# Order of the roundings at the heads of the stages, a shorter choice of expert groups, the first weight chunk in halves, and bias transfers one per chunk

## What is computed

```python
def first_block(x, ...):                       # per layer
    x = x + 0.5 * swiglu(rms_norm(x, ffn1_norm), w_gate, w_up, w_down)        # hidden width 2816
    h = rms_norm(x, mix_norm)
    ... = split(h @ w_in)                      # 5656 columns
    y_nsa = nsa_attention(...)                 # compressed, selected, windowed, with the relative bias
    y_sb  = stick_breaking_attention(...)
    y_swa = swa_sink_attention(...)            # with the relative bias
    x = x + (g0 * (y_nsa @ w_up_nsa) + g1 * (y_sb @ w_up_sb) + g2 * (y_swa @ w_up_swa)) @ w_out
    x = x + 0.5 * swiglu(rms_norm(x, ffn2_norm), ...)

def second_block(x, mem, ...):                 # per layer
    h = concat(gla_group(x @ w_in ...), sgu_group(...)) @ w_out
    x = layer_norm(DN_ALPHA * x + h)
    x = layer_norm(DN_ALPHA * x + mem_xattn(x, mem, wq, wk, wv, wo))
    x = layer_norm(DN_ALPHA * x + grouped_moe(x, ...))

def grouped_moe(x, w_router, b_router, w_gate, w_up, w_down):
    scores = softmax(x @ w_router + b_router)  # 16 experts in 4 groups of 4
    group_score = sum of the two largest scores of each group
    g_sel = argmax(group_score)                # the first of equal ones
    top_w, top_i = top_k(scores of the group g_sel, 2); top_w = top_w / sum(top_w)
    y = sum over the two experts: top_w * (silu(x @ w_gate[e]) * (x @ w_up[e])) @ w_down[e]
```

## Time and profile before

| | us |
|---|---|
| runs | 2324.76, 2325.26, 2319.07 |
| median | 2324.76 |
| the profiled execution | 2323.54 |
| its span in the trace | 2321.7 |
| PE busy | 2270.3 |
| DVE busy | 1598.3 |
| ACT busy | 1245.1 |
| POOL busy | 48.4 |

### The profile page before, as it was taken

The page is one execution under the profiler, slowest core; times in us unless marked ns, Lnnn a source line. Parts: engine busy times, 40 slices in busy tenths (PEclk is TensorE's granted clock), DMA queues, the critical chain, the costliest instruction groups (busy, mean ns, idle before and its releaser), DMA issues.

```text
span 2321.7 us, 31646 instructions
## 1 busy us (share of the span) xinstructions
PE 2270.3 (98%) x13500; PEld 1974.2 (85%) x13500; DVE 1598.3 (69%) x1535; ACT 1245.1 (54%) x1272; POOL 48.4 (2%) x67
## 2 busy tenths in 40 slices
PE   7999999999999999999999999999999999899998
PEld 6888989788888889897888999888888998688886
DVE  5765755777477558556764656688887666688887
ACT  4444634554354446444443545577776545467775
POOL 1000100000000001000000000000000000000000
PEclk9999999999999999999999999999999999899999
DMA  9655443456555554445655554599997554599995
GB/s 236 199 185 178 147 136 130 156 187 194 182 181 182 190 172 129 148 145 170 193 182 189 172 180 165 174 342 348 369 345 278 173 182 147 184 346 344 347 370 184
DMA packets 309793, 490.96 MB, mean 211 GB/s; under 512 B 15472, under 2 KB 205088, under 8 KB 309648
## 3 DMA queue, kind: packets, MB, share of 16 engines
q1 hardware_dynamic: 305696, 475.35, 60.9%
q0 software_dynamic: 3104, 10.38, 1.8%
q10 hardware_dynamic: 848, 3.15, 0.4%
HBM read 487.40 MB, written 1.44 MB: 211 GB/s over the span
## 4 chain that ended last, share of the span: by engine, by line
PE 92%; DVE 4%; ACT 2%; issue 1%; DMA 1%; ACTq 0%; DVEq 0%
PE PS L679 20%; PE PS L680 20%; PE PS L683 19%; PE PS L752 13%; PE PS L755 7%; PE PS L1372 1%; ACT RH L1532 1%; PE PS L975 1%; PE PS L940 1%; DVE RL L2024 1%; DMA RINGS<-ffn_w_up 1%; PE PS L914 1%; PE PS L699 1%; PE PS L925 1%; DVE X L2393 1%
## 5 line engine op out<-in xcount | busy, mean ns | idle before, releaser
L2024 DVE TENSOR_TENSOR RL<-RINGS,RH 128x2048 fp32r<-128x2048 f32 x448 | 1017.3, 2273 | 487.3 <-ACT RH L1532 484.8
L1532 ACT ACTIVATE RH<-RINGS 128x2048 fp32r<-128x2048 f32 x448 | 850.7, 1900 | 474.1 <-PE PS L683 449.6
L679 PE MATMUL PS<-RH,HTS 128*128 128x256 f32 (+1 forms) x1696 | 548.3, 334 | 0.4 <-DVE HTS L2006 0.4
L680 PE MATMUL PS<-RH,HTS 128*128 128x256 f32 (+1 forms) x1696 | 537.8, 328 | 0.0
L752 PE MATMUL PS<-HTS,RH 128*128 128x512 f32 x1384 | 416.7, 397 | 7.4 <-ACT RH L1532 7.4
L683 PE MATMUL PS<-RL,HTS 128*128 128x256 f32 (+1 forms) x1696 | 400.0, 326 | 0.0
L679 PEld LDWEIGHTS PS<-RH,HTS 128*128 128x128 f32 x1696 | 320.4, 189 | 32.6 <-issue 2.5
L680 PEld LDWEIGHTS PS<-RH,HTS 128*128 128x128 f32 x1696 | 321.5, 190 | 28.0
L683 PEld LDWEIGHTS PS<-RL,HTS 128*128 128x128 f32 x1696 | 289.5, 189 | 31.1 <-DVE RL L2024 0.4
L752 PEld LDWEIGHTS PS<-HTS,RH 128*128 128x128 f32 x1384 | 249.0, 189 | 55.6 <-issue 6.2
L755 PE MATMUL PS<-HTS,RL 128*128 128x256 f32 x1408 | 284.3, 281 | 0.4 <-DVE RL L2024 0.4
(11 more groups left out here) (434 smaller groups left out, 2534.7 us busy)
## 6 DMA issues: line engine op xcount, KB each, us to landing
RINGS<-w_in SPq DMA_DIRECT2D x64, 1024.0 KB, 5.3
RINGS<-w_gate SPq DMA_DIRECT2D x64, 1024.0 KB, 5.3
RINGS<-w_up SPq DMA_DIRECT2D x64, 1024.0 KB, 5.3
RINGS<-w_down SPq DMA_DIRECT2D x64, 1024.0 KB, 5.3
RINGS<-ffn_w_gate SPq DMA_DIRECT2D x44, 1024.0 KB, 5.4
RINGS<-ffn_w_up SPq DMA_DIRECT2D x44, 1024.0 KB, 5.3
RINGS<-ffn_w_down SPq DMA_DIRECT2D x44, 1024.0 KB, 4.9
RINGS<-w_out SPq DMA_DIRECT2D x16, 1024.0 KB, 4.9
```

Source lines behind the costliest of these rows:

```text
L679: mm(dst, a_[0], b_[0], start=start, stop=False)
L680: mm(dst, a_[0], b_[1], start=False, stop=False) if left else mm(dst, a_[1], b_[0], start=False, stop=False)
L1532: A(splits.buffer(RH, RH3)[:, 0:width], RINGS[:, slot, 0:width], ACT.Copy).then_inc(wh_ready, 1)
L2024: TTn(RL[:, slot, 0:width], RINGS[:, slot, 0:width], splits.buffer(RH, RH3)[:, 0:width].bitcast(F32), ALU.subtract).then_inc(wl_ready, 1)
```

## The change

1. **Start.** The first chunk is loaded in two transfers: k = 0..3 (`first_loaded`) and k = 4..7 (`ring_full[0]`). DVE rounds the first half itself, ahead of its activation rests, and raises `first_rounded`; ACT rounds only the second half (`split_first`). PE waits for `first_rounded` at k = 0 and for `wh_ready` at k = 4. ACT runs a Silu on one number after issuing x.
2. **Bias.** Each of the eight transfers waits for one more chunk done, from the seventh on. The row of the bias is made ahead of PE's other small products, so that one semaphore serves both.
3. **Rows of X in halves.** Row tile 1 is written as columns 0..511 (`x_left`) and 512..1023 (`x_rows`), at all places; PE's transposes of tile 1 wait for `x_left`, and for `x_rows` ahead of the third bank.
4. **Layer columns.** In block 1 those of layer 1 are copied within the second feed-forward stage of layer 0. In block 2, the copy and two memsets stand behind the activation rests and a weight split.
5. **Roundings.** At the head of the memory attention of layer 1 and of both routings, ACT does its activation copies ahead of one of the roundings that stood before them.
6. **Routing.** The group is chosen by maxima and minima of the exponentials as they are, without the division; the comparisons come behind `oh_ready`, the gates between the seats of groups 1 and 2. The seats of group 0 need one linked step less.
7. **End.** Row tile 1 is stored in two transfers of 256 KB.

```diff
@@ SP, load
+                if ring.n == 1:
+                    dst, half = shape_fn(RINGS[:, slot, :]), K // 2
+                    sp.dma_start(dst[:, 0:half, :], src[:, 0:half, :]).then_inc(first_loaded, 16)
+                    sp.dma_start(dst[:, half:K, :], src[:, half:K, :]).then_inc(ring_full[slot], 16)
+                    return
@@ POOL
                     for q in range(0, P, COPIES):
+
+                        pool.wait_ge(chunks_done, SLOTS + 7 + q // COPIES)
                         nc.gpsimd.dma_start(BIAS[q:q + COPIES, :, :], ...)
@@ PE, to_column_parts
-                pe.wait_ge(wh_ready, splits.v + splits.n)
+                opening = ring.n == 1
+                if opening:
+                    pe.wait_ge(first_rounded, 1)
+                else:
+                    pe.wait_ge(wh_ready, splits.v + splits.n)
...
                     for k in range(K - 1):
+                        if opening and k == K // 2:
+                            pe.wait_ge(wh_ready, splits.v + splits.n)
@@ PE, transpose_halves
-                pe.wait_ge(rows, first + 1)
+                if left is not None:
+                    pe.wait_ge(*left)
+                else:
+                    pe.wait_ge(rows, first + tail)
                 for b in range(4):
-                    if b == 2 and parts:
-                        pe.wait_ge(rows, first + 2)
+                    if b == 2 and left is not None:
+                        pe.wait_ge(rows, first + tail)
@@ ACT
+            def split_first():
...
+                act.wait_ge(ring_full[slot], ahead.full())
+                act.wait_ge(first_rounded, 1)
+                A(splits.buffer(RH, RH3)[:, half:SLOT], RINGS[:, slot, half:SLOT], ACT.Copy).then_inc(wh_ready, 1)
...
+            act.wait_ge(zeroed, 2)
+            A(EPS[:, 1:2], EPS[:, 0:1], ACT.Silu)
...
                     split()
-                    split(back=3)

                 ht_copy(tr2(l, 3), HT)
+                split(back=3)
                 chunk()
...
+            act.wait_ge(x_left, last_rows + 1)
+            act.dma_start(out_view[:, 1, 0:512], X[:, 1, 0:512]).then_inc(out_stored, 16)
+            act.wait_ge(x_rows, 2 * last_rows + 2)
+            act.dma_start(out_view[:, 1, 512:D], X[:, 1, 512:D]).then_inc(out_stored, 16)
@@ DVE
+                if l + f == 0:
+                    dve.wait_ge(first_loaded, 16)
+                    V.tensor_copy(RH[:, 0, 0:SLOT // 2], RINGS[:, 0, 0:SLOT // 2]).then_inc(first_rounded, 1)
                 ht_copy(tr1(l, 4 * f), HT, gains, bank=low)
...
-                V.scalar_tensor_tensor(X[:, 1, :], half_rows(1, low), SMALL[:, 7:8], X[:, 1, :], ALU.mult, ALU.add).then_inc(x_rows, 1)
+                for at, made in ((0, x_left), (512, x_rows)):
+                    part = X[:, 1, at:at + 512]
+                    V.scalar_tensor_tensor(part, half_rows(1, low)[:, at:at + 512], SMALL[:, 7:8], part, ALU.mult, ALU.add).then_inc(made, 1)
```

More of the change, by code:

```diff
@@ L818, in transpose_rows, with transpose_halves @@
                     last.then_inc(tr_ready, 1)
-            def transpose_halves(src, n, rows, first, upper=None, bank=0, parts=False):
+            def transpose_halves(src, n, rows, first, left=None, tail=1, upper=None, bank=0):
                 pe.wait_ge(ht_l, n * 4 + 4)
@@ L871, in swiglu @@
                     pe.wait_ge(consts_loaded, 16 * NLOAD)
+                    mm(PS[0:12, low + 3, :], RB, HOTR, start=True, stop=True)
                 for t in range(T):
@@ L874, in swiglu @@
                 last.then_inc(spread_ready, 1)
-                if l + f == 0:
-                    mm(PS[0:12, low + 3, :], RB, HOTR, start=True, stop=True).then_inc(hot_ready, 1)
                 for j in range(1, FP):
@@ L2594, in _ @@
                 dve.wait_ge(rt_exp, l + 1)
-                link(V.tensor_reduce(SMALL[:, 374:376], r3, AX.X, ALU.add))
-                link(V.reciprocal(SMALL[:, 376:378], SMALL[:, 374:376]))
-                link(TTn(r3, r3, spread(SMALL[:, 376:378], 2, NE), ALU.mult))
+                pairs = R.rearrange("p (g j i) -> p g j i", j=2, i=2)
+                top, low = (RTC[:, 16 * i:16 * i + 16].rearrange("p (g j) -> p g j", j=2) for i in range(2))
+                first, less, rest, second = (RTC[:, 32 + 8 * i:40 + 8 * i] for i in range(4))
+                TTn(top, pairs[:, :, :, 0], pairs[:, :, :, 1], ALU.max)
+                link(TTn(low, pairs[:, :, :, 0], pairs[:, :, :, 1], ALU.min))
+                TTn(first, top[:, :, 0], top[:, :, 1], ALU.max)
+                TTn(less, top[:, :, 0], top[:, :, 1], ALU.min)
+                link(TTn(rest, low[:, :, 0], low[:, :, 1], ALU.max))
+                link(TTn(second, less, rest, ALU.max))
+                link(TTn(SMALL[:, 448:456], first, second, ALU.add))
+                gs = SMALL[:, 448:456].rearrange("p (t g) -> p t g", t=2)
+                link(V.tensor_reduce(SMALL[:, 456:458], gs, AX.X, ALU.max))
+                eq = SMALL[:, 460:468].rearrange("p (t g) -> p t g", t=2)
+                before = RTN.rearrange("p (t g) -> p t g", t=2)
+                TTn(eq, gs, spread(SMALL[:, 456:458], 2, 4), ALU.is_equal)
+                link(TTn(before[:, :, 1], gs[:, :, 0], SMALL[:, 456:458], ALU.is_equal))
+                TTn(before[:, :, 2], eq[:, :, 0], eq[:, :, 1], ALU.max)
+                link(V.tensor_reduce(before[:, :, 3], eq[:, :, 0:3], AX.X, ALU.max))
+                TTn(OH, eq, before, ALU.is_gt).then_inc(oh_ready, 1)
                 r4 = R.rearrange("p (g i) -> p g i", i=4)
@@ L2646, in _ @@
                 for g in range(1, NG_):
-                    seats(g)
+                    if g == 2:
+                        gates()
+                    seat(g, 1)
+                    seat(g, 0).then_inc(seat_ready, 1)
                 wait_apart(dve, crowd_known, l + 1, consts_loaded, 16 * NLOAD)
```

105 lines of the change are left out of this document (56 added, 49 removed).

## The result

| | runs | median us | mean us | lowest to highest us |
|---|---|---|---|---|
| before | 5 | 2323.66 | 2322.7 | 2319.07 to 2325.26 |
| changed | 5 | 2309.93 | 2309.6 | 2308.47 to 2310.14 |

The ratio of changed to before is 0.9947, with a 95% interval of 0.9936 to 0.9958: the changed kernel is 10 to 15 us faster. The forecast was 2314.0, the range 2309.0 to 2320.5. The direction is right, and the time lies in the range, but near its lower end. By the medians the gain is 13.7 us, 3.5 more than the sum of 10.2, and more than the sum of the upper bounds, 12.7.

A forecast was written before the change was run, and what follows sets the result against it. PE, busy 98% of the span, bounds the kernel, so only its 51.4 us idle can shrink. Terms 2.0 + 3.3 + 2.3 + 1.9 + 0.65 = 10.2 us gave 2313.3 to 2314.6, stated 2314.0; range 2309.0 to 2320.5.

The forecast's parts named there:

- sum of 10.2: Whole kernel: gains of 2.0 start, 3.3 bias, 2.3 stage heads, 1.9 layer 1 routing and 0.65 tail, in us.
- Start, 2.0: First chunk: PE starts near 9.75, products with the rest begin at 14.4 instead of 16.88; 2.0 us gained.
- case (a): Rival at the start, chance 0.22: low PE clock takes gain back, start worth 1.0 instead of 2.0; time 2316.
- Bias, 3.3: Bias transfers spread one per load from chunk 7: PE no longer falls dry, 3.3 us gained, bounds 2.3 and 3.3.
- slack of 14.9 us: Weight stream: a load may take about 14.9 us before PE waits.
- price per transfer, 1.5: Bias transfers: eight cost a load 11.9 us, so one costs 1.5 and a load takes 6.8.
- 124 us for the table's first use: Mixer: bias table first used some 22 chunks in, at about 124 us, after the spread transfers end near 94.
- Heads, 2.3: Stage heads and layer 0 routing: halved rows, moved columns and ACT's earlier copies gain 2.3 us.
- the expected 0.5: Head of block 2 at 1269.15: PE's wait of 0.50 us goes entirely.
- Routing of layer 1, 1.9: Block 2 routing: gather starts 2.3 to 2.5 us earlier, of which 1.9 is kept because DVE isn't free as early.
- a wait of 3.5 instead of 5.0 leaves that as it is: Layer 1 gather: it ran at the low clock (granted 0.50), and PE's shorter wait was to leave that unchanged.
- Tail, 0.65: Last store: half its bytes go ahead, 0.75 less for moving, 0.1 more for the halved write; bounds 0 and 1.0.

The follow-up runs named there:

- 3.5 alone: Kernel before with one edit, each bias transfer waiting for one more chunk done, from the seventh on; median 2319.11 us; the trace has PE 3.5 us ahead.
- 3.8 when taken out: Changed kernel with the eight bias transfers back to back again; median 2315.32 us; 3.8 us lost at this place in the trace.
- the fours: Changed kernel with four bias transfers issued at the end of chunk 7 and four at chunk 8, instead of one per chunk; median 2312.07 us.

## Why the prediction came out as it did

- **Start, 2.0 of bounds 1.0 to 2.9.** The mechanism and each time of it were right to 0.25 us. The case (a), which I gave 0.22, happened in the profile of the changed kernel, or a little worse, and the gain at the full clock, 2.2, in three others. The 0.6 of the bad case lies below my lower bound of 1.0: I had priced the slow first seven products (1.4), which cost nothing, and not the eight with the rests (0.8) and those behind them up to 18.6 us (1.1). What the Trainium skill says of the clock (TensorE: Matmul & The Clock Gate, "What's actually happening"), that activity releases the low rate, is what these traces show at the start. An earlier start did bring the full rate earlier, at 8.1 to 13.5 us instead of 17.1, but in five of eight profiles it fell again near 11.8. That the clock could fall again there stood in none of the cases.
- **Bias, 3.3.** Right: 3.3 between the profiles, 3.5 alone, 3.8 when taken out. The slack of 14.9 us was right too. The price per transfer, 1.5, was too low, as the fours showed; it did no harm because 7.4 is still far below 14.9. The 124 us for the table's first use left out the 11 down chunks of the first stage: the mixer begins only at 201. That did no harm either. The 1.0 us that I had worked out with the rule from the Trainium skill (DMA: Bandwidth & Descriptors, "Queues, rings and completion order") is further off still, against 2.1 measured.
- **Heads, 2.3 of bounds 1.0 to 3.0.** Measured 3.2, above the upper bound. The mis-sized term is that of the five heads: 0.15 each where 0.34 was measured. PE wasn't held by 0.15 there: the whole write held it until 1.34 us after its start, the half lets it go after 1.04, and ACT's copies follow that. At 1269 the expected 0.5 was only 0.05: PE's wait for DVE went, and a new one of 0.48 for ACT's copies stood right behind it. The routing of layer 0 gave 0.6 for 0.34.
- **Routing of layer 1, 1.9 of 1.2 to 2.5.** Measured 1.4. The wait for the choice fell by 1.8 (worked out 1.5), the one linked step less in the first seat gave 0.12 (worked out 0.25), and the gather began 2.5 earlier. DVE, for which I had taken 0.5 off, wasn't what held the products behind it: there is no wait ahead of 2002.10. The step that failed is "a wait of 3.5 instead of 5.0 leaves that as it is", said of the gather's clock. The low stretch at the gather was as long as before (10.2 us, from 2003.6 and now from 1991.5). Before, the gather began 6.1 us into it and had 4.1 us of it left; now it begins 4.1 us into it and has 6.2 left.
- **Tail, 0.65.** Measured 0.5.
- **The sum, 10.2.** Without the low stretches the parts measured give 0.6 + 3.3 + 3.2 + 1.4 + 0.5 = 9.0, or 10.6 with the start at the full clock. The fastest of all runs of each kernel, 2317.82 and 2307.78, are 10.0 apart, though on different chips. The medians are 13.7 apart. The 3 to 4 us between are the size of the low stretches, 3.3 against 1.5 on average in the profiles. The prediction had no term for them, and took the one profile's time as if it had none. So the sum of 10.2 is close to what the parts give, but partly because the heads' 0.9 too little stands against 0.5 too much in the routing and up to 1.4 in the start.

## What to carry to other kernels

Where PE is busy 98% of the time, a short wait is also a chance that the clock falls behind it, at 1.5 us apiece here, and a run of very small products without any wait can be one too. So one profile is not enough to price a microsecond: compare the same instruction in both traces, count the low stretches apart, and run enough executions to see the levels. A transfer that isn't urgent should go beside the stream one at a time, and its price is to be read with the stream's slack (here 14.9 us for a 1 MB load), not from the bytes. Before shortening a chain in front of PE, look at what stands behind it on the engine that feeds PE next, and at the clock that PE will have when it gets there.

## What the runs showed of the hardware

- The same code had the granted clock at 0.50 from 11.8 to 18.5 us in five profiles and full there, from 13.5 us at the latest, in three; the places of low stretches within one kernel's middle part differ between executions, and each such stretch of 3.4 us costs 1.5.
- Of the 26 low stretches at the five places in fourteen profiles, fourteen came behind PE's waits of 1.43 and 0.67 us, one behind a wait of 1.44, and eleven with no wait of 0.05 us or more in the 40 us before, at the end of 32 products of 15 columns each.
- With products of a constant in PE's waits of the routing, the low stretches there (13.7 us in the changed kernel) were gone in one profile, and down to one of 3.4 us behind a wait of 1.94 us that was left unfilled in another.
- A 192 KB transfer whose rows in HBM are 1 KB each, beside a 1 MB load, takes 7.0 us and makes the load 2.1 us longer (7.4 against 5.3). With four and four, the load in the middle took 16.4; with eight back to back, 17.2 and 18.4.
- DVE's cast of 128x1024 from float32 took 0.69 us, less than twice the 0.427 of 128x512.
